# Dense expert sums accumulated in the banks by TensorE and carried by ScalarE, GpSimd's gathers written out, and the late tokens' gates held stationary

## The reference

```
q = (tb @ wq).reshape(.., 8, 2, 128);  s = einsum("thid,hikd->thik", q, keys)
sv, si = top_k(s, 16);  comb = sv[..0, :, None] + sv[..1, None, :]      # 16 x 16 candidates a head
fv, fi = top_k(comb, 16);  eidx = take(comb_idx, fi);  w = softmax(fv)  # 8 heads x 16 experts a token
act = gelu(einsum("thkd,td->thk", u[eidx], tb))
out = einsum("thk,thkd->td", w * act, v[eidx])
x = x + gate2 * out
```

## Time and profile before

| what | us |
|---|---|
| median of 3 runs | 4871.53 |
| lowest and highest | 4870.77, 4876.87 |
| the profiled execution's own time | 4885.86 |
| its span, first to last instruction | 4883.7 |
| TensorE busy | 4508.2 (92%) |
| VectorE busy | 3520.8 (72%) |
| ScalarE busy | 1813.4 (37%) |
| GpSimd busy | 1518.7 (31%) |

### The profile page before, as it was taken

How to read it: one execution, slowest core, us unless ns; L and a number is a source line. 1 busy time by engine, 2 the same in 40 slices (tenths; PEclk the granted TensorE clock), 3 DMA queues, 4 the chain that set the end, 5 groups by cost and what they waited for, 6 DMA issues and landing times. The chain is left out here.

```text
span 4883.7 us, 82658 instructions
## 1 busy us (share of the span) xinstructions
PE 4508.2 (92%) x28695; PEld 4184.8 (86%) x28695; DVE 3520.8 (72%) x6718; ACT 1813.4 (37%) x3800; POOL 1518.7 (31%) x1358
## 2 busy tenths in 40 slices
PE   7999999799989899969885769999999999999996
PEld 5999999799975598968774669999999999999995
DVE  3101555466754333447999979999999999999998
ACT  3111333244435431234444963333333333333332
POOL 0000000011110000000000017777777777777773
PEclk9999999899988899979997999999999999999998
DMA  4332222344433244338995569999999999999996
GB/s 164 107 139 97 82 91 87 124 141 140 146 110 58 63 166 184 135 116 306 345 330 197 206 240 364 361 372 371 371 376 372 374 362 371 370 372 377 377 370 248
DMA packets 351143, 1170.28 MB, mean 240 GB/s; under 512 B 40160, under 2 KB 91808, under 8 KB 344608
## 3 DMA queue, kind: packets, MB, share of 16 engines
q0 software_dynamic: 147456, 536.94, 29.2%
q1 hardware_dynamic: 160544, 483.06, 27.7%
q10 hardware_dynamic: 43008, 148.53, 8.1%
HBM read 971.20 MB, written 197.46 MB: 239 GB/s over the span
## 5 line engine op out<-in xcount | busy, mean ns | idle before, releaser
L2291 POOL DMA_INDIRECT ex_vr<-in_expert_v,ex_at x512 | 639.5, 1249 | 236.7 <-issue 150.3
L2289 POOL DMA_INDIRECT ex_ur<-scr_u_rows,ex_at x512 | 570.1, 1114 | 278.2 <-issue 118.1
L2478 DVE SCALAR_TENSOR_TENSOR ex_acc_rows<-ex_vr,ex_wt,ex_acc_rows 128x1024 f32<-128x1024 f32 x512 | 648.9, 1277 | 1.1 <-ACT ex_wt L2394 0.2
L2470 DVE SCALAR_TENSOR_TENSOR ex_ur<-ex_ur,h_rows 128x1024 f32<-128x1024 f32 x512 | 615.9, 1217 | 33.5 <-DMA ex_ur<-scr_u_rows,ex_at 32.6
L2283 POOL COPY ex_at<-picked_at 128x4 uint32 x128 | 96.3, 752 | 1469.0 <-POOLq L125 1468.5
L990 POOL TENSOR_TENSOR sd_cts<-sd_cT,sd_ea 128x512 f32<-128x512 f32 x72 | 98.5, 1368 | 1262.4 <-ACT sd_ea L880 1262.4
L2301 PE MATMUL ex_ps<-hd_hi,ex_u_hi 128*128 128x320 f32 x2048 | 470.4, 311 | 20.9 <-PEq L125 16.4
L2301 PE MATMUL ex_ps<-hd_lo,ex_u_hi 128*128 128x320 f32 x2048 | 470.0, 311 | 0.0
L2301 PE MATMUL ex_ps<-hd_hi,ex_u_lo 128*128 128x320 f32 x2048 | 469.1, 310 | 0.0
L2392 ACT ACTIVATE ex_gel<-ex_dot 128x1 f32<-128x1 f32 x512 | 103.6, 202 | 897.8 <-DVE ex_ur L2470 897.8
L479 DVE TENSOR_TENSOR pr_w_lo<-pr_w,pr_w_hi 128x1024 fp32r<-128x1024 f32 x56 | 68.6, 1226 | 489.4 <-ACT pr_w_hi L475 489.4
(11 more groups left out here) (365 smaller groups left out, 11142.9 us busy)
## 6 DMA issues: line engine op xcount, KB each, us to landing
pk_raw_u<-in_expert_u SPq DMA_DIRECT2D x128, 512.0 KB, 6.5
scr_u_rows<-pk_rows_u ACTq DMA_DIRECT2D x128, 512.0 KB, 6.2
ex_u<-in_expert_u SPq DMA_DIRECT2D x128, 512.0 KB, 6.8
ex_v<-in_expert_v SPq DMA_DIRECT2D x128, 512.0 KB, 8.4
scr_gate<-gt_stage SPq DMA_DIRECT2D x10, 4096.0 KB, 12.6
ex_gate<-scr_gate SPq DMA_DIRECT2D x32, 1280.0 KB, 8.7
pr_w<-in_w_main SPq DMA_DIRECT2D x58, 512.0 KB, 4.6
scr_xbc<-pr_out ACTq DMA_DIRECT2D x32, 576.0 KB, 3.8
```

Of the source, the lines that this page charges most:

```text
L2289: nc.gpsimd.indirect_dma_start(out=ur[:, s], out_offset=None, in_=scr["u_rows"], in_offset=by).then_inc(ur_in[s], 16)
L2291: nc.gpsimd.indirect_dma_start(out=vr[:, s], out_offset=None, in_=io["expert_v"].rearrange("j i d -> (j i) d"), in_offset=by).then_inc(vr_ ...
L2470: v.scalar_tensor_tensor(out=ur[:, s], in0=ur[:, s], scalar=1.0, in1=rows[:, s], op0=ALU.mult, op1=ALU.mult, accum_out=dot[:, m:m + 1]).th ...
L2478: v.scalar_tensor_tensor(out=acc_g[:, s], in0=vr[:, s], scalar=wt[:, m:m + 1], in1=acc_g[:, s], op0=ALU.mult, op1=ALU.add).then_inc(row_r[ ...
```

## The change

There are three parts, and one that follows from them.

GpSimd's loop is written out: 1024 gathers in a row, which read their indices straight from `picked_at` and wait on constants. The two copies of each pick and the helper's increments are gone. ScalarE's `weigh` reads its factor from `picked_share` at a place that depends on the loop's register.

The pieces change. Blocks 4 to 7 are computed for the first 512 tokens only, as four pieces of 6 products of 512 columns (`wide_tokens`), into one of two banks `ex_pv`. The last 128 of the 640 tokens get pieces of their own, j = 4 and 5 (`late_tokens`): there the gates of 128 tokens are the stationary operand and 512 columns of `v` the moving one, so that their output has tokens along the partitions. `ex_kept_late` is gone, and the six sums live in `ex_acc` (6 x 512).

The sums are carried by ScalarE. Before a piece, `give_sums(j)` copies the old sum from `ex_acc` into the bank, TensorE adds on top of it, and `take_sums(j)` copies the bank back. `add_sums` on VectorE is gone. In a batch, `give_sums(j + 2)` follows `take_sums(j)` on ScalarE, `take_sums(5)` and `give_sums(1)` stand at the head of the next batch, ahead of `round_v`, and `give_sums(0)` of the next batch ahead of `weigh(7)`.

In `finish_output` the four tiles to be turned for each of 8 blocks become five, and the shares of the dense and the turned tokens are 512 and 512 in place of 640 and 384.

```diff
-            ps, pv = pb2("ex_ps", [P, 2, 512]), pb2("ex_pv", [P, 512])
-            kept, kept_late = pb2("ex_kept", [P, KEPT, WIDE]), pb2("ex_kept_late", [P, KEPT, LATE])
+            ps, pv = pb2("ex_ps", [P, 2, 512]), pb2("ex_pv", [P, 2, WIDE])
+            kept = pb2("ex_kept", [P, KEPT, WIDE])
...
-                with pool.Fori(0, BATCHES) as b:
-                    for h in range(2):
-                        for s in range(ST):
-                            pool.wait_ge(row_r[s], b * 2 + h + START)
-                        nc.gpsimd.tensor_copy(at_now[:, h], at[:, :, ds(b * 2 + h, 1)].rearrange("p s j -> p (s j)")).then_inc(now_r, 1)
-                        nc.gpsimd.tensor_copy(share_now[:, h], share[:, :, ds(b * 2 + h, 1)].rearrange("p s j -> p (s j)")).then_inc(now_r, 1)
-                        free(now_r, b * 4 + (h + 1) * 2 + START)
...
+                for n in range(2 * BATCHES):
+                    for s in range(ST):
+                        by = bass.IndirectOffsetOnAxis(ap=at[:, s, n:n + 1], axis=0)
+                        pool.wait_ge(dot_r[s], n + START)
+                        nc.gpsimd.indirect_dma_start(out=ur[:, s], ...).then_inc(ur_in[s], 16)
+                        pool.wait_ge(row_r[s], n + 2 * START)
+                        nc.gpsimd.indirect_dma_start(out=vr[:, s], ...).then_inc(vr_in[s], 16)
...
+                def wide_tokens(out, d, r, first, last):
+                    for e in range(E):
+                        for x, y in SPLIT:
+                            mm = nc.tensor.matmul(out, v2[x][:, e, d * P:(d + 1) * P], g2[y][:, r, e, 0:WIDE],
...
+                def late_tokens(out, half, r, first, last):
+                    for e in range(E):
+                        for x, y in SPLIT:
+                            mm = nc.tensor.matmul(out, g2[y][:, r, e, WIDE:TD], v2[x][:, e, half * WIDE:(half + 1) * WIDE],
...
+                def piece(b, j, r):
+                    pe.wait_ge(given, b * SUMS + j + 1 + START)
+                    if j < KD - KEPT:
+                        last = wide_tokens(pv[:, j % 2], KEPT + j, r, False, True)
+                    else:
+                        last = late_tokens(pv[:, j % 2], j - (KD - KEPT), r, False, True)
+                    last.then_inc(sum_mm, 1)
...
+                    for d in range(KEPT):
+                        wide_tokens(kept[:, d], d, r, first, last)
+                        piece(b, d, r)
+                        u_products(2 * d, 2 * d + 1)
+                    for j in range(KD - KEPT, SUMS):
+                        piece(b, j, r)
...
+                def give_sums(b, j, first=False):
+                    if not first:
+                        act.wait_ge(sum_r, b * SUMS + j - 1 + START)
+                    nc.scalar.copy(pv[:, j % 2], sums[:, j]).then_inc(given, 1)
+                def take_sums(b, j):
+                    act.wait_ge(sum_mm, b * SUMS + j + 1 + START)
+                    nc.scalar.copy(sums[:, j], pv[:, j % 2]).then_inc(sum_r, 1)
...
-                def add_sums(b, j):
-                    a = (j % 2) * HW
-                    dve.wait_ge(sum_mm, b * SUMS + j + 1 + START)
-                    v.tensor_tensor(acc[:, j // 2, a:a + HW], acc[:, j // 2, a:a + HW], pv[:, 0:HW], ALU.add).then_inc(sum_r, 1)
```

More of the change, by code:

```diff
@@ L2304, in u_product @@
                         last.then_inc(mm[e], 1)
[L2306 removed]
+                def wide_tokens(out, d, r, first, last):
                     for e in range(E):
                         for x, y in SPLIT:
[L2310 to L2318 removed]
+                            mm = nc.tensor.matmul(out, v2[x][:, e, d * P:(d + 1) * P], g2[y][:, r, e, 0:WIDE],
+                                                  start=first and e == 0 and (x, y) == SPLIT[0], stop=last and e == E - 1 and (x, y) == SPLIT[-1], skip_group_check=True)
+                    return mm
+                def late_tokens(out, half, r, first, last):
                     for e in range(E):
                         for x, y in SPLIT:
[L2321 to L2322 removed]
+                            mm = nc.tensor.matmul(out, g2[y][:, r, e, WIDE:TD], v2[x][:, e, half * WIDE:(half + 1) * WIDE],
+                                                  start=first and e == 0 and (x, y) == SPLIT[0], stop=last and e == E - 1 and (x, y) == SPLIT[-1], skip_group_check=True)
+                    return mm
+                def piece(b, j, r):
[4 more added lines that the diff above has]
+                        last = late_tokens(pv[:, j % 2], j - (KD - KEPT), r, False, True)
                     last.then_inc(sum_mm, 1)
@@ L2430, in _ @@
                 batch(BATCHES - 1, 1, False, False)
-                act.wait_ge(sum_mm, BATCHES * SUMS + START)
+                take_sums(BATCHES - 1, 5)
+                act.wait_ge(sum_r, BATCHES * SUMS + START)
                 for s in range(ST):
                     act.wait_ge(dot_r[s], BATCHES * 2 + START)
-                nc.scalar.copy(early[:, :, 0:WIDE], kept[:])
-                nc.scalar.copy(early[:, :, WIDE:TD], kept_late[:]).then_inc(early_r, 1)
+                nc.scalar.copy(early, kept[:]).then_inc(early_r, 1)
             @block.vector
@@ L2540, in _, with finish_output @@
                 dve.wait_ge(early_r, 1 + START)
-        finish_output(nc, io, per, scr, [early[:, k] for k in range(KEPT)] + [acc[:, k] for k in range(KD - KEPT)], acc_g, x_first, x_in, fg)
-def finish_output(nc, io, per, scr, acc, acc_g, x_first, x_in, fg):
-    LP = SEQ - TD
+        finish_output(nc, io, per, scr, [early[:, k] for k in range(KEPT)] + [sums[:, k] for k in range(KD - KEPT)], (sums[:, KD - KEPT], sums[:, KD - KEPT + 1]), acc_g, x_first, x_in, fg)
+def finish_output(nc, io, per, scr, acc, late_sums, acc_g, x_first, x_in, fg):
+    WIDE = TD - P
+    LP = SEQ - WIDE
     with ExitStack() as ctx:
@@ L2604, in turn @@
                     pe.wait_ge(x_r, k - 1 + START)
+                half, at = k // (KD // 2), k % (KD // 2) * P
+                nc.tensor.transpose(pst[:, k % 2, 0:P], late_sums[half][:, at:at + P], ident)
                 for s in range(ST):
-                    last = nc.tensor.transpose(pst[:, k % 2, s * P:(s + 1) * P], acc_g[:, s, k * P:(k + 1) * P], ident)
+                    last = nc.tensor.transpose(pst[:, k % 2, (s + 1) * P:(s + 2) * P], acc_g[:, s, k * P:(k + 1) * P], ident)
                 last.then_inc(turned, 1)
```

86 lines of the change are left out of this document (31 added, 55 removed).

## The result

The changed kernel takes 4828.8 us (median of 4, 4819.7 to 4834.6) beside 4874.2 for the kernel before on the same chip. The ratio is 0.9905, 95% interval 0.9889 to 0.9921: some 45 us faster, where 101 were forecast. 4829 lies in the wide range of the prediction (4735 to 4852), but outside the forecast's own case A (4738 to 4801). The profiled execution took 4833.9, span 4832.1, against 4885.9 and 4883.7.

A forecast was written before the change was run, and what follows sets the result against it. TensorE, VectorE and DMA were taken as full at once; afterwards TensorE's 27.9 us plus 0.5 lateness gave 28.4 a batch against 29.98. Saving 1.58 times 63, 99.5, plus 2 at the ends took 4871.5 to 4770, range 4735 to 4852.

The forecast's parts named there:

- case A: The forecast: experts' stretch at 28.4 us a batch, 4770 us, 4738 to 4801, DMA 390 to 400 GB/s; chance 0.57.
- 27.9 of TensorE: TensorE's work in a batch of the experts' stretch after the change: 27.9 us, 1.3 less than 29.2.
- 0.5 of lateness: Waits for late transfers in the experts' batches, added to TensorE's work: 0.5 us a batch, between 0 and 1.1.
- a period above 29: Sign on the mean time between batches' first kept products: above 29 us, or below 27.8, the forecast is wrong.
- waits for `ex_ur`: Sign on VectorE's waits for gathered rows of u: 20 to 50 us for case A, over 80 for Rival C.
- Rival C: Bytes bound the experts' stretch: DMA engines give no more than 375 GB/s, 29.7 us a batch, 4853 us; chance 0.15.
- 26.4 forecast: VectorE's work in a batch: eight additions of 3.2 us in all go, 29.6 becomes 26.4.
- ScalarE and its ring: ScalarE: copies 0.6 us, busy 17.4 a batch; loop of VectorE's dots, ScalarE's copies and rounding of v closes at 27.8.
- the heavy batch: DMA in every second batch, which also moves gates: 11.8 MB, needing 28.6 us at 412 GB/s.
- the light one: DMA in a batch without gates: 10.5 MB, needing 25.5 us at 412 GB/s.
- I costed it at 0: GpSimd's removed copies and earlier gathers: worth 0, at most 0.2 us a batch.
- rival D: Slower: GpSimd's straight code stalls gathers by fetching; one stall in each batch makes 4968 us; chance 0.11.

The follow-up runs named there:

- e12_floor: Changed kernel with ScalarE rounding v before the sum copies, the next batch's gelu ahead of weigh 0 and 1, and gathers fetching half rows; 4746 us, ratio 0.9740.
- e9_half: Changed kernel with each gather fetching half rows (512 numbers instead of 1024), as many gathers; 4793 us, ratio 0.9828.
- e7_more: Changed kernel with one more 524 kB store to unused memory in 58 of the 64 batches; 4877 us, ratio 1.0005.
- e2_bytes: Changed kernel loading only half of each u and v tile of the experts, 1.05 MB a batch less; 4799 us, ratio 0.9834.
- e15_bytes11: Changed kernel with ScalarE rounding v before the sum copies, gelu ahead of weigh 0 and 1, and half u and v tiles loaded; 4766 us, ratio 0.9761.
- e8_straight: Kernel before with only GpSimd's gathers written out, without copies, and weigh reading shares through a register; sums and products as before; 4844 us, ratio 0.9932.
- e4_loop: Changed kernel with GpSimd's loop, its copies and weigh of the kernel before; 4907 us, ratio 1.0074.
- e5_lesspe: Changed kernel without TensorE's product with the low part of u, 4.7 us of its work a batch; 4827 us, ratio 0.9891.
- e16_ring: Changed kernel with gathers fetching half rows and without TensorE's product with the low part of u; 4753 us, ratio 0.9738.

## Why the prediction was wrong

**What the sum had wrong.** The forecast was 27.9 of TensorE and 0.5 of lateness, 28.4 a batch; measured are 29.31, of which TensorE's part is 27.8. So one term carries the whole miss: 1.5 where 0.5 stood. The signs that the prediction named point the same way: a period above 29, 158 us of waits for `ex_ur` (over 80 was the sign for C), and 372 to 384 GB/s in the windows where A had 390 to 400.

**TensorE: right.** 27.9 was forecast, 27.8 is measured where nothing else binds (e12_floor), with 0.23 for wide and late pieces alike.

**VectorE: right.** 26.4 forecast; 227 of 250 us at 29.31 are 26.6. It frees no bank any more, and TensorE's waits for it are gone but for `ex_g_lo`.

**ScalarE and its ring: right.** Copies 0.58 and 0.59 against 0.6, busy 146 / 250 x 29.31 = 17.1 against 17.4, ring 28.03 against 27.8. The rule of the Trainium skill (ScalarE: Activation LUTs, Step-by-step: what each stage is for) that writing to PSUM is the faster way makes no difference of use here: into the bank 591 ns, out of it 583, and the cast within SBUF of the earlier trace rows, another instruction, 613. One thing was not priced: the gelu of the next batch stands behind weigh 0 and 1, and TensorE waits 0.5 a batch for it. By e9_half and e12_floor it and the two copies ahead of the rounding of v are worth 28.64 - 27.85 = 0.8, with rows in time.

**DMA: the step that failed, by its size.** I wrote that at 412 GB/s the heavy batch needs 28.6 and the light one 25.5, and added 0.5 a batch. 412 is the rate of windows with gates; the light batch can't have it. The row itself said so: at 353 GB/s the share was 0.96, which makes 368 at a full share, and 412 at 1.02 makes 404. Then the light batch takes 10.5 MB / 368 = 28.5, the heavy one 11.8 / 404 = 29.2, on average 28.9. The window of 250 us says it at once: 375 at 0.98 is 383, and 11.14 MB at that are 29.1. The queues of the changed kernel from 3000 to 4500 (packets, MB, share of 16 engines) agree:

```profile
q0 software_dynamic: 117728, 428.66, 74.6%
q1 hardware_dynamic: 33330, 141.30, 24.3%
```

The gathers (q0) at 428.66 / (1500 x 0.746) = 383 GB/s, everything at 570.0 / (1500 x 0.989) = 384: 29.0 for 11.14 MB. With e7_more's 389 it is 28.6. So instead of 27.0 with a little lateness, bytes stood at 28.6 to 29.0, above TensorE and the ring. (Such a quotient holds for one mix of transfers: the same division gives 368 in e2_bytes and 332 in e9_half.) That no single one of them sets the period is shown by the sensitivities: neither 4.7 us of TensorE's work, nor 1.2 us of ring, nor an earlier gather moved it by more than some 0.2, 1.05 MB less moved it 0.57, and both kinds of cut together 1.23 (e15_bytes11). Limits of 27.8 (TensorE), 28.0 (ring) and 28.6 to 29.0 (bytes) lie side by side, with GpSimd's 25.6 not far below. That a late row is not made up by the next is the likely reason for the rest; it is not shown. Rival C had the mechanism (chance 0.15) and its waits of over 1 us a batch came (2.5), but its rate, 375, is that of a share of 0.98, short of full, and gave 4853.

The rule of the Trainium skill (DMA: Bandwidth & Descriptors, Where 436 GB/s comes from) that transfers from HBM to SBUF are held at about 358 GB/s would have made it an estimated 31.1; the trace disagrees, with 382 in the changed kernel and 391 in e7_more's window.

**GpSimd: the other step that failed.** I costed it at 0, since "None of it was on the path by itself". It doesn't enter the 28.4, so it isn't what made the number wrong; wrong was where the gain comes from. Most of it came from here (e8_straight), and it makes the rest possible: with its old loop beside the new sums it needs 29.9 a batch, and that is slower than the kernel before. I had looked at when gathers start, never at how much of the batch GpSimd is occupied. By its lines it was taken for 27.6 of 29.98 in the kernel before: fuller than its busy 185 of 250 says, as its gaps between gathers are its own. The rival D, stalls from straight code, didn't happen: of 1024 gathers one took over 2.5 us (5.8), where the loop before had 14 of 4.9. I had taken the one of the earlier trace rows for a single case and thought of fetched code; VectorE's operations beside it explain its length.

GpSimd's 0.48, where 0 to 0.2 stood, was a gain that could be had alone; behind it the sums, worth 1.6 by TensorE's work (29.50 to 27.9), found room for 0.2 (29.50 to 29.31).

What stays open: which part of e8_straight's 33 us came from the copies and which from the loop's long gathers. In the trace of the kernel before, undisturbed batches take 29.45; of the 33 us above that, 20 lie in the 26 batches that hold or follow a gather of over 2.5 us, and 13 in the other 36, so such gathers aren't all of it. (e4_loop has the same loop and none of these.) Open is also which part of the last 0.3 to 0.7 above the bytes' own time comes from late rows that VectorE can't make up, and which from the DMA engines' idle moments between gathers. Another buffer for rows of u would tell; it wasn't tried.

## What to carry to other kernels

Divide a rate by its share before using it as a capacity, and do it window by window, for the mix of transfers that the kernel will have: 353 at 0.96 is not a batch with room, it is a batch at 368. Count an engine that issues work by its busy time and its own gaps together; one that seems 74% busy can be 92% taken. When three resources are within 4%, price a change to two of them as what the third leaves, not as what the two save.

## What the runs showed of the hardware

GpSimd's small copies are dear: 128x4 numbers took a mean of 0.5 to 0.8 us for indices and 0.9 to 1.1 for shares, and two per half batch cost this kernel 61 us. Its gathers took 0.94 us when VectorE was idle, read its accumulator or added from the bank, and otherwise until some 0.8 behind the end of VectorE's operation, mostly up to 1.98 and in rare cases 4.9 or 5.8; half the bytes made them no shorter (a busy 202 of 250 in e9_half's windows, 183 in the changed kernel's). Fewer bytes do not free the DMA engines in proportion: with half rows the gathers of e9_half moved 219.17 MB at 44.8% of 1500 us, 326 GB/s where it had been 383, so a cut by half saved 40% of the engines' time. TensorE's granted clock went to 0.92 in the windows of e5_lesspe and e16_ring, where it idled 33 and 26 us of 250, and stayed at 1.00 with the 9 of the changed kernel.
